# Encoder kernel: reordering the mixing stage (both K tiles first, squares on ScalarE, Q and V scaled on VectorE)

## What is computed

```python
h = _rmsnorm(x, mix_norm[l])
p = h @ w_mix_in[l]                       # columns: u, v (512 each), q (512), k, v (128 each)
# gating, 4 groups of 128 channels
z = gelu(a_proj); u, v = split(z)
v = _rmsnorm(v per group, norm_g)
s = einsum('gpq,bcqgd->bcpgd', w_s, vc) + b_s
out_a = u * s
# attention, 8 query heads on 2 key heads of 64, window of 128
q = _rmsnorm(q per head, q_g); k = _rmsnorm(k per head, k_g)
s = q k^T / 8 + bias; m = max(s, sink); p = exp(s - m); p = p / (sum(p) + exp(sink - m))
out_b = p v
x = x + concat(out_a, out_b) @ w_mix_out[l]
```

## Time and profile before

| | us |
|---|---|
| median of 3 runs | 942.89 (942.44 to 945.35) |
| the profiled execution, its own time | 945.81 |
| its span, first to last instruction | 944.1 |
| PE busy | 923.9 |
| DVE, ACT, POOL busy | 516.0, 436.9, 92.4 |

### The profile page before, as it was taken

One profiled execution on the slowest core, in us unless ns is written; L12 is line 12 of the kernel. 1 busy time (PEld: TensorE's weight loads), 2 busy tenths in 40 slices (PEclk: granted clock), 3 DMA queues, 4 the chain that ended last, 5 costly groups with the idle time before them and its releaser, 6 DMA issues.

```text
span 944.1 us, 13030 instructions
## 1 busy us (share of the span) xinstructions
PE 923.9 (98%) x4434; PEld 768.6 (81%) x4434; DVE 516.0 (55%) x574; ACT 436.9 (46%) x515; POOL 92.4 (10%) x140
## 2 busy tenths in 40 slices
PE   8999999998999999999989999999989999999997
PEld 6888888886888888888878888888868888888886
DVE  5654554566666644455456444464757674554542
ACT  6453443455745434345355343452656463433421
POOL 5000000115400000000010000000434000000000
PEclk9999999999999999999999999999999999999999
DMA  8999999744154674654546745645431566564521
GB/s 268 275 178 263 173 232 225 215 143 168 46 175 153 221 239 147 203 197 155 167 142 234 239 156 195 208 141 201 148 135 36 188 196 205 178 214 161 188 105 44
DMA packets 119320, 168.97 MB, mean 179 GB/s; under 512 B 5805, under 2 KB 98025, under 8 KB 119273
## 3 DMA queue, kind: packets, MB, share of 16 engines
q1 hardware_dynamic: 117408, 163.60, 51.2%
q0 software_dynamic: 1504, 4.73, 7.3%
q10 hardware_dynamic: 360, 0.03, 0.0%
HBM read 165.19 MB, written 3.14 MB: 178 GB/s over the span
## 4 chain that ended last, share of the span: by engine, by line
PE 90%; POOL 4%; issue 2%; DVE 2%; DMA 1%; ACT 0%; POOLq 0%; ACTq 0%; SPq 0%; DVEq 0%
PE U L910 18%; PE U L913 18%; PE U L911 18%; PE D L910 5%; PE D L911 5%; PE D L913 5%; PE C L910 5%; PE C L911 5%; PE C L913 5%; PE TR L965 2%; POOL rstd L402 2%; PE TR L1044 1%; PE D L1075 1%; DMA raw<-in_ffn_w_in_dram 1%; POOL mean L401 1%
## 5 line engine op out<-in xcount | busy, mean ns | idle before, releaser
L662 DVE TENSOR_TENSOR w_lo<-raw,w_hi 128x2048 fp32r<-128x2048 f32 (+1 forms) x154 | 346.4, 2269 | 122.3 <-ACT w_hi L475 122.2
L910 PE MATMUL U<-w_hi,xT_hi 128*128 128x512 f32 (+1 forms) x784 | 309.2, 394 | 3.2 <-issue 2.6
L475 ACT ACTIVATE w_hi<-raw 128x2048 fp32r<-128x2048 f32 (+1 forms) x154 | 287.5, 1894 | 50.4 <-DMA raw<-in_ffn_w_in_dram 29.8
L913 PE MATMUL U<-w_hi,xT_lo 128*128 128x512 f32 (+1 forms) x784 | 304.7, 389 | 0.0
L911 PE MATMUL U<-w_lo,xT_hi 128*128 128x512 f32 (+1 forms) x784 | 303.9, 388 | 0.0
L910 PEld LDWEIGHTS U<-w_hi,xT_hi 128*128 128x128 f32 x784 | 148.6, 190 | 32.0 <-issue 3.0
L913 PEld LDWEIGHTS U<-w_hi,xT_lo 128*128 128x128 f32 x784 | 148.5, 189 | 30.6
L911 PEld LDWEIGHTS U<-w_lo,xT_hi 128*128 128x128 f32 x784 | 148.7, 190 | 28.3
L491 ACT ACTIVATE hT_hi<-TR 128x256 fp32r<-128x256 f32 x88 | 29.4, 382 | 240.1 <-PE TR L965 240.1
L674 DVE TENSOR_TENSOR hT_lo<-TR,hT_hi 128x256 fp32r<-128x256 f32 x88 | 33.6, 419 | 164.8 <-ACT hT_hi L491 164.8
L487 ACT ACTIVATE small<-U,inv 128x256 f32<-128x256 f32 x88 | 41.8, 475 | 115.9 <-PE D L913 79.0
(11 more groups left out here) (119 smaller groups left out, 770.5 us busy)
## 6 DMA issues: line engine op xcount, KB each, us to landing
raw<-in_ffn_w_in_dram SPq DMA_DIRECT2D x176, 512.0 KB, 4.8
raw<-in_ffn_w_out_dram SPq DMA_DIRECT2D x88, 512.0 KB, 5.2
raw<-in_w_mix_in_dram SPq DMA_DIRECT2D x28, 512.0 KB, 4.6
raw<-in_w_mix_out_dram SPq DMA_DIRECT2D x16, 512.0 KB, 3.7
bias_rows<-o POOLq DMA_DIRECT2D x8, 255.5 KB, 11.3
bias<-bias_rows POOLq DMA_DIRECT2D x8, 192.0 KB, 6.0
xs<-in_x_dram SPq DMA_DIRECT2D x2, 512.0 KB, 6.5
out_dram<-xs SPq DMA_DIRECT2D x4, 256.0 KB, 2.0
```

Source lines behind the costliest of these rows:

```text
L475: act.activation(w_hi[:, p % SLOTS, a:], raw[:, p % RAW, a:], ACT.Copy).then_inc(hi_ready, 1)
L662: dve.tensor_tensor(w_lo[:, p % SLOTS, a:], raw[:, p % RAW, a:], w_hi[:, p % SLOTS, a:].bitcast(F32), ALU.subtract).then_inc(lo_ready, 1)
L910: pe.matmul(out_, x_hi, w_hi[:, slot, c], start=start, stop=False)
L913: last = pe.matmul(out_, x_lo, w_hi[:, slot, c], start=False, stop=stop)
```

## The change

Four things are done in the mixing stage of both layers. The order becomes K0, K1, Q0, Q1, V0, V1, in `FILLS`, `TAKEN`, `NORMED` and in every engine's program. The squares of K and Q are made by ACT straight from the PSUM bank, with the inverse norm as scale, right behind the `take`; those of V by ACT from the taken tile. Q and V are scaled by DVE (`scale_q` in one instruction, `scale_v` in four), and POOL keeps only the mean and the power. The splits of the V, U and output weights stand later in DVE's order, and V0 and V1 are taken earlier and apart in ACT's. On PE the second tile's KV projection goes ahead of the second half of Q0, k1's transposes ahead of the second half of Q1, scores 0 ahead of the second half of V0, scores 1 ahead of the second half of V1, and scores 2 ahead of the first half of U0.

```diff
-TAKEN = ["KV0", "Q0", "KV1", "Q1", "V0", "V1", "U0", "U1"]
-NORMED = ["K0", "Q0", "K1", "Q1", "V0", "V1"]
+TAKEN = ["KV0", "KV1", "Q0", "Q1", "V0", "V1", "U0", "U1"]
+NORMED = ["K0", "K1", "Q0", "Q1", "V0", "V1"]
...
                 for t in range(2):
-                    squares(L, f"K{t}", kv[:, t, 0:2 * HD], 2 * HD)
-                    norm(L, f"K{t}", 2 * t, 2, HD).then_inc(rstd_done, 1)
-                    squares(L, f"Q{t}", qs[:, t, :], MIX_A)
-                    step(norm(L, f"Q{t}", 4 + 8 * t, NH, HD), L)
...
+                    norm(L, f"K{t}", 2 * t, 2, HD)
                 for t in range(2):
+                    norm(L, f"Q{t}", 4 + 8 * t, NH, HD)
+                for t in range(2):
+                    norm(L, f"V{t}", 20 + 4 * t, NG, P)
...
+            def take_squares(L, name, n):
+                t = int(name[-1])
+                if name == "K0":
+                    act.wait_ge(ms_done, n_inv(L, 1, 1))
+                else:
+                    act.wait_ge(sums_done, n_of(L, NORMED, NORMED[NORMED.index(name) - 1]))
+                act.activation(sq[:, 0:n], PROJ_BANK[name.replace("K", "KV")][:, 0:n], ACT.Square,
+                               scale=inv[:, t:t + 1]).then_inc(sq_done, 1)
+            def squares_v(L, t):
+                act.wait_ge(sums_done, n_of(L, NORMED, NORMED[NORMED.index(f"V{t}") - 1]))
+                act.wait_ge(proj_taken, n_of(L, TAKEN, f"V{t}"))
+                act.activation(sq[:, :], gv[:, t, :], ACT.Square).then_inc(sq_done, 1)
...
+            def scale_q(L, t):
+                dve.wait_ge(rstd_done, n_of(L, NORMED, f"Q{t}"))
+                qv = qs[:, t, :].rearrange("p (h d) -> p h d", h=NH)
+                dve.tensor_tensor(qv, qv, rstd[:, 4 + 8 * t:12 + 8 * t].unsqueeze(2).to_broadcast([P, NH, HD]),
+                                  ALU.mult).then_inc(q_normed, 1)
+            def scale_v(L, t):
+                dve.wait_ge(rstd_done, n_of(L, NORMED, f"V{t}"))
+                for g in range(NG):
+                    cols = slice(g * P, (g + 1) * P)
+                    last = dve.scalar_tensor_tensor(out=gv[:, t, cols], in0=gv[:, t, cols],
+                                                    scalar=rstd[:, 20 + 4 * t + g:21 + 4 * t + g],
+                                                    in1=sgain[:, cols], op0=ALU.mult, op1=ALU.mult)
+                last.then_inc(v_normed, 1)
```

PE's new order, from the second half of Q0 on:

```diff
-                project(L, POS_Q + 1, 0, 1, C0[:, :], MIX_A).then_inc(proj_ready, 1)
                 project(L, POS_KV, 1, 0, U[1][:, 0:4 * HD], 4 * HD)
+                project(L, POS_Q + 1, 0, 1, C0[:, :], MIX_A).then_inc(proj_ready, 1)
...
                 project(L, POS_Q, 1, 0, C1[:, :], MIX_A)
+                pe.wait_ge(k_normed, L * 2 + 2)
+                fill(L, "k1", [kd[:, 1, g, :] for g in range(2)])
                 project(L, POS_Q + 1, 1, 1, C1[:, :], MIX_A)
                 pe.wait_ge(q_normed, L * 2 + 1)
                 fill(L, "q0", tiles(qs, 0))
...
                 project(L, POS_V, 0, 0, U[0][:, :], MIX_A)
-                pe.wait_ge(k_normed, L * 2 + 2)
-                fill(L, "k1", [kd[:, 1, g, :] for g in range(2)])
+                pe.wait_ge(tr_dve, n_of(L, BY_DVE, "q0"))
+                pe.wait_ge(sq_done, n_of(L, NORMED, "Q1"))
+                scores(L, 0)
                 project(L, POS_V + 1, 0, 1, U[0][:, :], MIX_A).then_inc(proj_ready, 1)
...
```

More of the change, by code:

```diff
@@ L77, in runs_of_buckets @@
     return [(int(rel[a]), int(rel[z - 1]) + 1, int(b[a])) for a, z in zip(cuts, cuts[1:])]
-FILLS = ["ws", "k0", "q0", "k1", "q1", "p0a", "p0b", "p1a", "p1b", "p2a", "p2b", "o0", "p3a", "p3b", "a0", "o1", "a1"]
+FILLS = ["ws", "k0", "k1", "q0", "q1", "p0a", "p0b", "p1a", "p1b", "p2a", "p2b", "o0", "p3a", "p3b", "a0", "o1", "a1"]
 BY_ACT = [n for n in FILLS if not n.endswith("b")]
@@ L406, in inverse_rms @@
                 rsqrt(L, inv[:, t:t + 1], ms[:, t:t + 1], mean[:, 30 + t:31 + t], D, 1).then_inc(inv_done, 1)
[L408 to L413, removed]
             def norm(L, name, c0, groups, n):
                 pool.wait_ge(sums_done, n_of(L, NORMED, name))
-                return rsqrt(L, rstd[:, c0:c0 + groups], sums[:, c0:c0 + groups], mean[:, c0:c0 + groups], n, groups)
+                rsqrt(L, rstd[:, c0:c0 + groups], sums[:, c0:c0 + groups], mean[:, c0:c0 + groups], n,
+                      groups).then_inc(rstd_done, 1)
             base = steps
@@ L599, in _ @@
                 take(L, "KV0", kv[:, 0, :], ACT.Copy, 4 * HD)
+                take_squares(L, "K0", 2 * HD)
                 split(L, POS_V)
-                take(L, "Q0", qs[:, 0, :], ACT.Copy, MIX_A)
                 evacuate(L, "ws", wsT[:, :])
@@ L604, in _ @@
                 take(L, "KV1", kv[:, 1, :], ACT.Copy, 4 * HD)
+                take_squares(L, "K1", 2 * HD)
                 split(L, POS_U)
+                take(L, "Q0", qs[:, 0, :], ACT.Copy, MIX_A)
+                take_squares(L, "Q0", MIX_A)
                 evacuate(L, "k0", kT_hi[:, :, 0:P], 2 * P, gcur[:, G_K:G_K + 1])
+                evacuate(L, "k1", kT_hi[:, :, P:2 * P], 2 * P, gcur[:, G_K:G_K + 1])
+                evacuate(L, "q0", qT_hi[:, 0, :, :], 512, gcur[:, G_Q:G_Q + 1])
                 take(L, "Q1", qs[:, 1, :], ACT.Copy, MIX_A)
-                evacuate(L, "q0", qT_hi[:, 0, :, :], 512, gcur[:, G_Q:G_Q + 1])
+                take_squares(L, "Q1", MIX_A)
                 split(L, POS_U + 1)
-                evacuate(L, "k1", kT_hi[:, :, P:2 * P], 2 * P, gcur[:, G_K:G_K + 1])
+                exps(L, 0)
                 evacuate(L, "q1", qT_hi[:, 1, :, :], 512, gcur[:, G_Q:G_Q + 1])
-                split(L, POS_OUT)
[L613 to L617, removed]
+                take(L, "V0", gv[:, 0, :], ACT.Gelu_apprx_tanh, MIX_A)
+                squares_v(L, 0)
+                exps(L, 1)
+                evacuate(L, "p0a", pT[:, 0, :])
+                take(L, "V1", gv[:, 1, :], ACT.Gelu_apprx_tanh, MIX_A)
+                squares_v(L, 1)
+                split(L, POS_OUT)
                 exps(L, 2)
@@ L621, in _ @@
                 exps(L, 3)
+                take(L, "U0", qs[:, 0, :], ACT.Gelu_apprx_tanh, MIX_A)
                 evacuate(L, "p2a", pT[:, 0, :])
-                take(L, "U0", qs[:, 0, :], ACT.Gelu_apprx_tanh, MIX_A)
                 evacuate(L, "o0", xT_hi[:, 4:8, 0:P])
@@ L854, in _ @@
                 sum_of(L, "K0", 0, 2, HD)
+                scale_k(L, 0)
                 split(L, POS_V)
-                scale_k(L, 0)
+                sum_of(L, "K1", 2, 2, HD)
+                scale_k(L, 1)
                 sum_of(L, "Q0", 4, NH, HD)
+                evacuate_lo(L, "k0", kT_lo[:, 0, :, :], kT_hi[:, :, 0:P], gcur[:, G_K:G_K + 1])
+                scale_q(L, 0)
+                evacuate_lo(L, "k1", kT_lo[:, 1, :, :], kT_hi[:, :, P:2 * P], gcur[:, G_K:G_K + 1])
                 split(L, POS_V + 1)
[L859 to L862, removed]
                 evacuate_lo(L, "q0", qT_lo[:, 0, :, :], qT_hi[:, 0, :, :], gcur[:, G_Q:G_Q + 1])
                 sum_of(L, "Q1", 12, NH, HD)
-                evacuate_lo(L, "k1", kT_lo[:, 1, :, :], kT_hi[:, :, P:2 * P], gcur[:, G_K:G_K + 1])
-                split(L, POS_U + 1)
-                evacuate_lo(L, "q1", qT_lo[:, 1, :, :], qT_hi[:, 1, :, :], gcur[:, G_Q:G_Q + 1])
                 dve.wait_ge(mix_params, L * 48 + 48)
@@ L870, in _ @@
                 biased(L, 0)
-                split(L, POS_OUT)
[L872 to L876, removed]
+                scale_q(L, 1)
+                split(L, POS_U)
+                evacuate_lo(L, "q1", qT_lo[:, 1, :, :], qT_hi[:, 1, :, :], gcur[:, G_Q:G_Q + 1])
+                split(L, POS_U + 1)
+                biased(L, 1)
+                sum_of(L, "V0", 20, NG, P)
+                evacuate(L, "p0b", pT[:, 1, :])
+                scale_v(L, 0)
+                biased(L, 2)
+                sum_of(L, "V1", 24, NG, P)
+                evacuate(L, "p1b", pT[:, 1, :])
+                scale_v(L, 1)
+                split(L, POS_OUT)
                 biased(L, 3)
-                sum_of(L, "V1", 24, NG, P)
                 attended(L, 0)
@@ L1131, in _ @@
                 fill(L, "q0", tiles(qs, 0))
[L1132 removed]
+                pe.wait_ge(sq_done, n_of(L, NORMED, "K0"))
                 project(L, POS_V, 0, 0, U[0][:, :], MIX_A)
[L1134 to L1135 removed]
+                pe.wait_ge(tr_dve, n_of(L, BY_DVE, "q0"))
+                pe.wait_ge(sq_done, n_of(L, NORMED, "Q1"))
+                scores(L, 0)
                 project(L, POS_V + 1, 0, 1, U[0][:, :], MIX_A).then_inc(proj_ready, 1)
[L1138 to L1140 removed]
                 pe.wait_ge(q_normed, L * 2 + 2)
@@ L1143, in _ @@
                 project(L, POS_V, 1, 0, U[1][:, :], MIX_A)
-                project(L, POS_V + 1, 1, 1, U[1][:, :], MIX_A)
                 pe.wait_ge(tr_dve, n_of(L, BY_DVE, "q1"))
                 scores(L, 1)
+                project(L, POS_V + 1, 1, 1, U[1][:, :], MIX_A)
                 probs_T(L, 0)
+                scores(L, 2)
```

(1 more changed line is left out.)

14 lines of the change are left out of this document (2 added, 12 removed).

## The result

The changed kernel takes **936.10 us** (median of 4 runs, 934.73 to 937.53), the kernel before 943.28 us (4 runs, 942.44 to 945.35). The ratio is 0.992, with a 95% interval of 0.9906 to 0.9934: faster by 7.2 us where 4.7 were forecast, and just under the lower end of the wide range, 936.2, and 0.7 us under the forecast's own, 936.8 to 941.0. In a later comparison it was 936.84 against 944.24 us, ratio 0.9922 (0.9908 to 0.9935), so the gain is nearer 7 than 4.7. The profiled execution after took 936.17 us by its own time, with a span of 934.5; the one before 945.81 and 944.1. The mixing stage of the first layer, from the first KV matmul to the first one of the output projection, took 64.58 us before (199.78 to 264.36) and takes 59.76 now (198.78 to 258.54). The second layer's went from 64.57 to 59.77 us.

A forecast was written before the change was run, and what follows sets the result against it. PE, busy 98% of the span, was the bound, losing only to idling and a slow clock. Per layer 1.04 + 1.6 - 0.1 - 0.2 = 2.3, both layers 4.7 us: from 942.89 to 938.2 us, range 936.8 to 941.0.

The forecast's parts named there:

- the wide range: Range of the kernel time over forecast and rivals, 936.2 to 942.6 us, leaving out under 0.2 of the chances.
- The power: POOL's power over eight columns in each Q chain, priced at 3.61 to 3.80 us, twice in the path.
- The new wait of 1.1 us at q0: PE, ready after k1's transposes, would wait 1.1 us per layer for scaled q0, where it waited for nothing.
- the old one of 1.75 at q1: PE would still wait 1.75 us for q1, due at 228.1 instead of 229.14: 1.04 us won per layer.
- a POOL mean waits for DVE: Rival: a POOL mean ahead of q1 takes 2.05 instead of 0.2 us, once per layer; 941.9 us, chance 0.08.
- k1: PE's wait for the scaled k1 tile, 1.35 us per layer, would go as K1's chain starts after the earlier KV1.
- Fewer stalls: Rival: POOL's start and DVE's sums come sooner at both Q tiles, 1 us per layer more; 936.2 us, chance 0.05.
- The clock: PE's clock would hold at 1.00 behind q1's transposes instead of falling to 0.50, winning 1.6 us per layer.
- The clock falls all the same: Rival: the clock still falls, 1.6 us lost per layer; 939.8 us for one layer, 941.4 for both, chance 0.25.
- ACT and weighted 1: ACT busy without pause for 11.3 us from second-round exponentials to p1a; PE loses 0.1 us per layer before weighted 1.
- Weighted 2: Needs p2a, now behind U0's take and its table, due at 253.5 against 253.4; 0.2 us lost per layer.
- The tables: Rival: ACT's table switches hold twice their 1.28 us load, 3.8 us lost per layer; 945.9 us, slower, chance 0.07.

## Why the prediction was wrong

- **The power, the step that failed.** The forecast took 3.61 us as the price of the power over eight columns ("the power, 3.61 to 3.80, twice in the path") and kept it in a kernel in which the splits moved away from it. It measured 1.64. Everything else in that chain held: with the stage starting 1.0 us sooner, the power was due at 214.05 and began at 214.01; the tile was due 1.97 us later than it came (218.35 against 216.38), and 3.61 - 1.64 is 1.97. The new wait of 1.1 us at q0 and the old one of 1.75 at q1 both hung on it, and neither came. Won were the whole 3.65 us of a layer's waits in place of 1.04, 5.2 us more in all. That this was the cause is shown from both sides: with the split put back the power is 3.61 and PE waits 1.0 us at q0, and the moved splits alone give 936.03.
- **What the forecast had seen.** It wrote that a mean took 2.05 us "while DVE was in a weight split", and priced the rival "a POOL mean waits for DVE". The same collision in the power stood in DVE's rows: the 3.80 and 3.61 began within 0.2 us of a split's start. The upper and lower bound of that price, 3.80 and 3.61, were both rows of a blocked instruction, so the bounds did not bound it.
- **The rule that would have told.** The Trainium skill (SBUF — State Buffer, Who interferes with whom) says that a DVE instruction with two SBUF inputs contends with a GpSimd instruction that reads SBUF, that whichever issues first blocks the other fully, and that a reduction never contends on this chip, nor an instruction with at most one SBUF input, unless it runs in one of DVE's 2-port modes. The traces agree: a power of 3.61 us beside two inputs against 1.64 beside the reduction, and a split of 2.88 us behind a multiplication that began first. A power that began first is the exception: a split met it and neither waited (the last section has the times). By the rule the 3.6 would have been read as work and wait.
- **k1.** Right: its 1.35 us went. But K1's chain before held two collisions that the forecast did not name as its cause: the mean, 2.05 us for 0.20, and DVE's scaling at 221.38, 1.25 us for 0.48, which began while POOL squared Q1 (221.32 to 222.36).
- **A slip in the sum.** The terms for q1 (223.25, 0.45, 3.61, 0.69) add up to 228.0, not 228.1. It is 0.1 us a layer and decides nothing.
- **The rivals' times.** "Fewer stalls" stood at 936.2, next to the measured 936.10. Its mechanism, POOL's start and DVE's sums coming sooner, is not what happened: the power's start was due at 214.05 and came at 214.01. That the number fits it is luck. "A POOL mean waits for DVE" did not come either: both means ahead of Q's powers took 0.20 us.
- **The clock.** The forecast's clock held in the stage, 1.00 there. The 1.6 us per layer are true of the profiled execution, but not of the medians: this second term was over-sized. Over their spans the runs of before have a mean granted clock of 0.9957, those after about 0.997, so by estimate some 4.1 us and 2.8 us are lost to the clock, and about 1.2 us are the gain, not 3.2. The single runs agree: of before, 0.993 goes with 945.2 to 946.9 us and 0.998 with 942.8 to 943.6. The profiled execution of before, at 0.994, was one with both falls.
- **The clock's rival.** "The clock falls all the same", at 1.1 and 1.75 us of idling: the kernel with two extra two-input instructions had that pattern (5.4 us in 4 waits, the longest 1.6) and no fall. There it held. But the ground that the forecast gave, that gaps shorter than a harmless one of 2.6 us do no harm, did not: with Q scaled by DVE, gaps of 0.66 and 1.92 us were followed by a fall in one layer. That the clock held in this stage was luck as much as reasoning.
- **ACT and weighted 1.** Right: from 231.45 to 242.54, 11.1 us against 11.3, and no wait against 0.1. All of it came some 4 us sooner than forecast, because q1 did.
- **Weighted 2.** Near: 0.46 us against 0.2, by the mechanism named, p2a behind U0's take and its table. It comes ahead of the transposes before weighted 2.
- **The tables.** Right, the rival is out: the loads are 1.28 us and the next instruction follows after 0.01. The Trainium skill's further 1.38 us of drain per switch (ScalarE: Activation LUTs, What ACT_TABLE_LOAD costs) do not show in this kernel: the load at 234.13 starts 0.02 us after the end of the evacuation before it. Four more switches in the two layers came with a gain.

By the forecast's own sum: 4.7 + 5.2 (the power) - 0.3 (weighted 1 and 2) - 2.0 (the clock) = 7.6 us, against 7.2 measured. Two errors of opposite sign partly hid each other; without the clock's, the forecast would have been further off.

## What to carry to other kernels

Before a duration is used as a price, look at what the other engines did in those microseconds, above all when the same operation shows two lengths, or one that is out of line with its size: eight columns at 3.6 us beside four at 1.0. Where GpSimd has a link in a chain that TensorE waits for, keep VectorE's long two-input instructions out from beside it; here the order of four calls was worth as much as the rewritten stage. And a wait that is taken away is only worth what lies up to the next engine's chain: the splits moved away from the powers gained 8.8 us, and one of them moved once more lost 3.0.

## What the runs showed of the hardware that was not expected

- The POOL instruction that meets a running two-input DVE instruction waits for its end and is recorded with the wait inside its duration: a power 3.61 to 3.80 us for 1.64, a mean 2.05 for 0.20, multiplications of 128x512 2.13 to 3.17 for 1.04, and V's second one (L458) 3.20 for 1.29. A POOL instruction already running is not lengthened.
- It goes the other way too. A split that begins while POOL multiplies a 128x512 tile takes the wait itself: 2.85 to 2.90 us for 2.28, in both layers of the kernel before and of three of the experiments' kernels. So does a DVE instruction with a single tensor input: the scaling of K1 takes 1.25 us for 0.48 wherever it begins behind POOL's squares of Q1, and 0.48 where ACT makes them.
- A power under way does not hold a split up: with the squares on ACT, splits began 1.1 and 0.7 us behind the start of a power, and both kept their times (2.28 and 2.29, 1.64 and 1.65 us).
- POOL's power costs 0.70, 1.01 and 1.64 us for two, four and eight columns, so its price rises with the columns.
- The clock does not fall by a fixed rule of gaps that these traces would show. With Q scaled by DVE, PE's waits were 0.66 and 1.92 us in both layers, to 0.01 us; the first layer then ran the 5 us from 228.00 at a mean of 0.66, the second the 6 us from 691.00 at 1.00. With the split one place later, 0.77 and 0.45 us were followed by 0.50 in the second layer and by 1.00 in the first. What decides between the two was not tried and stays open; for a forecast it means that a fall is a chance, to be priced by the mean clock of several runs and not by one profile.
